# Two-block hybrid layer, dilated groups: value projection first in natural token tiles, through DRAM, ahead of keys and queries

## The chip, the cores and the metric

The kernel runs on one core of one Trainium2 chip. The metric is the device time of one execution in microseconds (us); lower is better. The kernel before takes 1719.8 us, the median of three runs (1716.84 to 1724.75).

## What is computed

The input is one sequence of 1024 tokens of width 1024, in float32. A first block (pooling and sliding-window attention) feeds a second, hybrid one. What matters here is the dilated attention of the second block: 24 heads of width 64 in three groups of eight. Queries, keys and values of a group are three slices of one projection, `h @ w_in`; queries and keys are rotated, values are not.

```
DIL_CONFIGS = ((128, 1), (512, 4), (2048, 16))

def dilated_mixture(q, k, v, positions):
    q = rope(q.reshape(B, S, DIL_HEADS, DIL_HEAD_DIM), positions)
    k = rope(k.reshape(B, S, DIL_HEADS, DIL_HEAD_DIM), positions)
    v = v.reshape(B, S, DIL_HEADS, DIL_HEAD_DIM)
    for g, (window, dilation) in enumerate(DIL_CONFIGS):
        sl = slice(g * DIL_HEADS_PER_GROUP, (g + 1) * DIL_HEADS_PER_GROUP)
        o, lse = dilated_group(q[:, :, sl], k[:, :, sl], v[:, :, sl], dilation, window // (2 * dilation))
    ...
    alpha = jax.nn.softmax(jnp.stack(lses, axis=0), axis=0)
    out = jnp.sum(alpha[..., None] * outs, axis=0)
```

In `dilated_group` a query sees the 64 keys of its own residue class on either side of it (dilation 1 or 4), or all 64 of its class (dilation 16).

## The kernel before, in words

The program is written by hand for the five engines, each with its own instruction stream and semaphores between them. Every float32 product is made of three passes: both operands are split into a high and a low part, and high times high, high times low and low times high are summed in PSUM.

The dilated part is a row of **units** (`D_UNITS`, L476). A unit is one 128x512 tile of a projection: 8 steps over the contraction, times three passes, so 24 matmuls, on TensorE (`d_proj`, L1172). For each group g there are eight units of keys, then those of values, then eight of queries. Keys and queries come out transposed (channels on partitions), 128 channels by 512 tokens. Values come out with tokens on partitions: the stationary operand is 128 columns of the transposed activations `h2T_hi` or `h2T_lo`, so the choice of columns chooses the tokens (`value_tiles`, L450). In group 0 the value tiles are shifted by 64 tokens against the query tiles, so that a query tile's window is two value tiles; that takes nine tiles for eight tiles' worth of tokens. In groups 1 and 2 a value tile's columns are taken with a step of 4 or 8 tokens.

A unit takes two **slots** (twelve matmuls each). `unit_before` (L508) tells which unit has just been finished at a slot. The three PSUM banks 0 to 2 take the units in turn (`d_bank`), and a unit waits until the one three before it has been read.

- A value unit is copied by ScalarE from PSUM to its tile in `v_dil` (L1756).
- A key or query unit is rotated. ScalarE copies it to `rope_in` (L1760). SyncE (SP) then issues four DMAs that write it to `rope_swapped` with 32-partition blocks exchanged (`swap_halves`, L599). VectorE multiplies the PSUM tile by the cosines into `kT_dil` or `qT_dil` (`rope_cos`, L2273), multiplies `rope_swapped` by the sines (L2280), and adds the two (`rope_sin`, L2284), which it tells by the semaphore `roped`. There is one `rope_in` and one `rope_swapped`: ScalarE's next copy waits for the swap before it, and the next swap waits for that add.

During the query units of a group the attention of that group runs in **steps** (`step_at`, L499), which begin `STEP_LAG` = 4 slots after the first query unit's own first slot: scores (`d_scores`, L1197), mask and maximum on VectorE, exponentials on ScalarE, transposes, and the product with the values (`d_values`, L1227, from `v_dil`). The last steps of a group lie beside the first three units of the next group. `d_scores` of a group's first step waits for `roped` of query unit 0 (groups 0 and 1) or 1 (group 2).

Weights come in **panels** of 512 columns, four chunks of 512 KB each. SP loads chunks (`load_chunk`, L630) into a ring of two, at the odd slots 1, 3, 5 and 7 of a panel; GpSimd splits each chunk into `w_hi` (L700) and `w_lo` (L707). There are two panels of split weights, so the splitting for the next panel begins when the one before the present is done, at the start of a panel of units. SP's stream is in program order: at the start of each panel it stands swap of the last unit, chunk load, swap of the next unit, chunk load, and so on.

After the dilated part the gates, the combination of the three groups, the latent attention and the output projections follow.

## Time and profile before

| what | before |
|---|---|
| median of the runs | 1719.8 us (1716.84 to 1724.75) |
| the profiled execution, its own time | 1716.44 us |
| its span from first to last instruction | 1714.6 us |
| TensorE matmul busy | 1686.5 us (98%), 8753 instructions |
| TensorE weight load busy | 1412.7 us (82%) |
| VectorE, ScalarE, GpSimd busy | 797.7, 586.1, 508.9 us |
| mean granted clock of TensorE | 0.999 of 2.4 GHz |

Of the 1716.44 us, 1.84 us lie around the span. The dilated units run from 558.75 us to about 1124 us of it. A busy matmul is not a matmul at its peak: the records overlap, so the pace is read from the distance of starts, not from durations.

### The profile page before, as it was taken

The numbers are of one execution on the slowest core, as the hardware profiler recorded it, in microseconds if no ns is written. First come the engines' busy times: TensorE is split into PE (matmuls) and PEld (weight loads), VectorE is DVE, ScalarE is ACT, GpSimd is POOL, SyncE is SP. The second block draws the span as 40 slices with busy tenths as digits, with TensorE's granted clock in tenths as the row PEclk, the third lists the DMA queues.
The fourth block names the chain that finished last, engine by engine and source line by source line (L and its number), as shares of the span: only waits on it lengthen the run. The fifth ranks groups of instructions, "written<-read, shape, count | busy, mean of one in ns | idle before, by whom it ended". The sixth has DMA issues, their size and how long they took to land.

```text
span 1714.6 us, 22451 instructions
## 1 busy us (share of the span) xinstructions
PE 1686.5 (98%) x8753; PEld 1412.7 (82%) x8753; DVE 797.7 (47%) x1214; ACT 586.1 (34%) x1337; POOL 508.9 (30%) x400
## 2 busy tenths in 40 slices
PE   7999999999999999999999999999999999999998
PEld 6778878889878787888978889788787999988886
DVE  4330366334342213554166541646521888855714
ACT  5101456334333102441134310442113777741211
POOL 6125033023333333021220223015313744534310
PEclk9999999999999999999999999999999999999999
DMA  6113022233267422113131232227465535226332
GB/s 205 50 65 108 13 62 70 87 119 93 74 215 269 117 62 59 50 50 85 56 84 38 72 83 60 69 54 267 137 227 164 139 63 139 53 68 212 107 114 98
DMA packets 99290, 178.20 MB, mean 104 GB/s; under 512 B 16200, under 2 KB 36080, under 8 KB 99056
## 3 DMA queue, kind: packets, MB, share of 16 engines
q1 hardware_dynamic: 63280, 95.31, 20.1%
q10 hardware_dynamic: 35904, 81.44, 13.5%
q8 instruction: 70, 1.15, 0.3%
q14 instruction: 36, 0.29, 0.1%
HBM read 115.49 MB, written 48.63 MB: 96 GB/s over the span
## 4 chain that ended last, share of the span: by engine, by line
PE 92%; DVE 2%; ACT 2%; DMA 1%; issue 1%; POOL 1%; SPq 1%; ACTq 0%; DVEq 0%; POOLq 0%
PE ps L1193 22%; PE ps L1107 15%; PE ps L813 13%; PE ps L1045 5%; PE ps L1360 5%; PE ps L1300 5%; PE ps L947 4%; PE ps L1241 4%; PE ps L1330 3%; PE ps L1313 3%; PE ps L868 3%; PE ps L1209 2%; PE ps L1222 2%; PE ps L999 2%; PE ps L972 1%
## 5 line engine op out<-in xcount | busy, mean ns | idle before, releaser
L700 POOL TENSOR_SCALAR w_hi<-w_stage 128x1024 fp32r<-128x1024 f32 (+3 forms) x140 | 127.5, 918 | 996.7 <-PE ps L1193 361.2
L707 POOL TENSOR_TENSOR w_lo<-w_stage,w_hi 128x1024 fp32r<-128x1024 f32 (+3 forms) x140 | 270.1, 1937 | 8.9
L1193 PE MATMUL ps<-h2T_hi,w_hi 128*128 128x512 f32 x384 | 156.7, 408 | 0.7 <-ACT gate_tiles L1608 0.7
L1107 PE MATMUL ps<-h2T_hi,w_hi 128*128 128x512 f32 x384 | 154.1, 401 | 0.5 <-issue 0.3
L1193 PE MATMUL ps<-h2T_hi,w_lo 128*128 128x512 f32 x384 | 152.2, 396 | 0.0
L1107 PE MATMUL ps<-h2T_lo,w_hi 128*128 128x512 f32 x384 | 151.8, 395 | 0.0
L1107 PE MATMUL ps<-h2T_hi,w_lo 128*128 128x512 f32 x384 | 151.6, 395 | 0.0
L1193 PE MATMUL ps<-h2T_lo,w_hi 128*128 128x512 f32 x384 | 151.3, 394 | 0.0
L1735 ACT ACTIVATE probs_dil<-probs_dil,dil_stats_out 128x256 f32<-128x256 f32 (+2 forms) x192 | 87.6, 457 | 137.1 <-DVE dil_stats_out L2301 137.1
L1300 PE MATMUL ps<-k_mla,q_mla 128*128 128x512 f32 x384 | 104.0, 406 | 0.0
L2393 DVE TENSOR_REDUCE small<-ps 128x1 f32<-128x1024 f32 x64 | 77.6, 1213 | 54.9 <-PE ps L1300 54.9
L2273 DVE SCALAR_TENSOR_TENSOR qT_dil<-ps,cos_table_T 128x512 f32<-128x512 f32 x24 | 23.1, 963 | 168.0 <-ACT rope_in L1760 168.0
L732 POOL TENSOR_SCALAR p_mla<-p_mla,small 128x1024 f32<-128x1024 f32 x64 | 71.7, 1120 | 88.1 <-DVE small L2386 87.9
L1193 PEld LDWEIGHTS ps<-h2T_hi,w_hi 128*128 128x128 f32 x384 | 72.1, 188 | 26.5 <-issue 9.2
L2380 DVE TENSOR_TENSOR pT_mla_lo<-ps,pT_mla_hi 128x512 fp32r<-128x512 f32 x128 | 81.9, 679 | 14.0 <-ACT pT_mla_hi L1848 14.0
L1848 ACT ACTIVATE pT_mla_hi<-ps 128x512 fp32r<-128x512 f32 x128 | 69.7, 596 | 52.1 <-PE ps L1313 52.1
L1107 PEld LDWEIGHTS ps<-h2T_hi,w_hi 128*128 128x128 f32 x384 | 72.2, 188 | 18.2 <-POOL w_lo L707 0.7
L1241 PEld LDWEIGHTS ps<-v_dil,probsT_dil 128*128 128x128 f32 (+1 forms) x640 | 80.6, 191 | 7.5 <-issue 1.1
L1193 PEld LDWEIGHTS ps<-h2T_hi,w_lo 128*128 128x128 f32 x384 | 72.2, 188 | 17.6
L1107 PEld LDWEIGHTS ps<-h2T_hi,w_lo 128*128 128x128 f32 x384 | 72.1, 188 | 17.6
L2280 DVE TENSOR_TENSOR rope_swapped<-rope_swapped,sin_table_T 128x512 f32<-128x512 f32 x48 | 43.6, 909 | 92.4 <-DMA rope_swapped<-rope_in 92.4
L1107 PEld LDWEIGHTS ps<-h2T_lo,w_hi 128*128 128x128 f32 x384 | 72.2, 188 | 16.3
(296 smaller groups left out, 3819.5 us busy)
## 6 DMA issues: line engine op xcount, KB each, us to landing
w_stage<-in_w_in SPq DMA_DIRECT2D x76, 512.0 KB, 3.9
rope_swapped<-rope_in SPq DMA_DIRECT2D x192, 64.0 KB, 2.0
w_stage<-in_w_out SPq DMA_DIRECT2D x16, 512.0 KB, 3.8
gate_scr<-gate_tiles ACTq DMA_DIRECT2D x16, 512.0 KB, 3.4
gates<-gate_scr ACTq DMA_DIRECT2D x32, 256.0 KB, 3.5
dil_scr<-dil_out SPq DMA_DIRECT2D x96, 64.0 KB, 1.6
dil_nums<-dil_scr ACTq DMA_DIRECT2D x24, 256.0 KB, 4.1
x_back<-in_x ACTq DMA_DIRECT2D x8, 512.0 KB, 3.9
```

The source lines that it names most:

```text
L700: last = nc.gpsimd.tensor_scalar(hi_, raw_, 1.0, 0.0, ALU.mult, ALU.add)
L707: last = nc.gpsimd.tensor_tensor(lo_, raw_, hi_.bitcast(F32), ALU.subtract)
L813: m = pe.matmul(acc, a, b, start=(i == 0 and j == 0), stop=(i == len(pairs) - 1 and j == 2))
L1045: m = pe.matmul(ps[:, Y_BANKS[t % 4] + half, :], a[:, k, tk], b[:, s, k, :], start=(k == 0 and j == 0), stop=(k == KT - 1 and j == 2))
L1107: m = pe.matmul(ps[:, gate_bank(u), :], a[:, s, k, P * m_:P * m_ + P], b[:, k, COLS * n:COLS * n + COLS], start=(k == 0 and j == 0), stop= ...
L1193: m = pe.matmul(bank, a, b, start=(k == 0 and i == 0), stop=(k == KT - 1 and i == 2))
L1241: m = pe.matmul(ps[:, 7, o:o + HD], pTd[r0:r0 + nr, c, :], vd[r0:r0 + nr, vt, HD * h:HD * h + HD], start=(kb == 0), stop=(kb == len(blocks ...
L1300: m = pe.matmul(ps[:, 2 * (i % 2) + n, :], Q[:, a, q], K[:, b, COLS * n:COLS * n + COLS], start=(j == 0), stop=(j == 2))
L1360: m = pe.matmul(ps[:, u % 8, :], a, b, start=(k == 0 and j == 0), stop=(k == 3 and j == 2))
L1735: act.activation(p_, p_, ACT.Exp, bias=o[:, h:h + 1], accum_out=o[:, H1 + h:H1 + h + 1]).then_inc(sem("d_exp"), 1)
L2380: nc.vector.tensor_tensor(PTl[dst], ps[:, 4 + half, :].rearrange("p (j c) -> p j c", c=P), PTh[dst].bitcast(F32), ALU.subtract).then_inc(s ...
L2393: nc.vector.tensor_reduce(rstd[:, j % 8:j % 8 + 1], ps[:, 2 * (j % 2):2 * (j % 2) + 2, :].rearrange("p b c -> p (b c)"), AX_X, ALU.max, ne ...
```

## The change

The order of a group is values, keys, queries. Value units are made in natural tiles (128 neighbouring tokens, 24 units in all instead of 25). ScalarE copies them to `rope_in` too. SP stores `rope_in` to a DRAM scratch `v_dil_scr` (256 KB, `store_values`), and ScalarE's next copy waits for that store. When all eight are stored, SP loads the tiles of `v_dil` that the attention reads from that scratch, one behind the swap of each key unit, with the shift or the step now in the rows that the load reads (`load_values`; 9, 8 and 8 loads of 256 KB). The first `d_values` of a group waits for these loads.

```diff
     for g in range(3):
+        add(f"v{g}", panel(w2, o_v + COLS * g))
         add(f"k{g}", panel(w2, o_k + COLS * g))
-        add(f"v{g}", panel(w2, o_v + COLS * g))
         add(f"q{g}", panel(w2, o_q + COLS * g))
...
+    vd_d = nc.dram_tensor("v_dil_scr", [S, 512], F32, kind="Internal").ap()
...
-    def value_tiles(g):
+    def value_rows(g):
 
         if g:
-            return [(t, group_toks(g, t)) for t in range(TT)]
-        starts = [0] + [P * t - HD for t in range(1, TT)] + [S - P]
-        return [(t, spread(s_, 1)) for t, s_ in enumerate(starts)]
+            return [tile_start(g, t) for t in range(TT)]
+        return [(0, 1)] + [(P * t - HD, 1) for t in range(1, TT)] + [(S - P, 1)]
...
-    D_UNITS = [(g, kind, t) for g in range(3) for kind in "kvq"
-               for t in range(len(value_tiles(g)) if kind == "v" else 2 * 4)]
+    D_UNITS = [(g, kind, t) for g in range(3) for kind in "vkq" for t in range(TT)]
...
+        def store_values(u):
+
+            g, _, t = D_UNITS[u]
+            sp.wait_ge(*after("d_read", u + 1))
+            if g and t == 0:
+                sp.wait_ge(*after("v_moved", 16 * (9, 17)[g - 1]))
+            sp.dma_start(vd_d[P * t:P * t + P, :], ts[:]).then_inc(sem("v_stored"), 16)
+
+        def load_values(u):
+
+            g, kind, t = D_UNITS[u]
+            for tile in range(t, TT + 1 if t == TT - 1 and g == 0 else t + 1):
+                sp.wait_ge(*after("v_stored", 16 * TT * (g + 1)))
+                if g:
+                    sp.wait_ge(*after("d_valued", d_step(g, 0)))
+                start, step = value_rows(g)[tile]
+                sp.dma_start(vd[:, tile, :], vd_d[start:start + step * (P - 1) + 1:step, :]).then_inc(sem("v_moved"), 16)
...
-            if done and done[3] != "v":
-                swap_halves(done[0])
+            if done:
+                (store_values if done[3] == "v" else swap_halves)(done[0])
+                if done[3] == "k":
+                    load_values(done[0])
...
                 if kind == "v":
-                    toks = value_tiles(g)[t][1]
-                    pairs = [(toks(a, k), b[:, s, k, :]) for a, b in ((h2h, wh), (h2h, wl), (h2l, wh))]
+                    pairs = [(a[:, k, P * t:P * t + P], b[:, s, k, :]) for a, b in ((h2h, wh), (h2h, wl), (h2l, wh))]
...
-                pe.wait_ge(*after("d_read", D_UNITS.index((g, "q", 0))))
+                pe.wait_ge(*after("v_moved", 16 * (9 + 8 * g)))
...
                 act.wait_ge(*after("d_done", u + 1))
-                if kind == "v":
-                    act.activation(vd[:, t, :], ps[:, d_bank(u), :], ACT.Copy).then_inc(sem("d_read"), 1)
-                else:
-                    if r:
-                        act.wait_ge(*after("swapped", 64 * r))
-                    act.activation(ts[:], ps[:, d_bank(u), :], ACT.Copy,
-                                   scale=HD ** -0.5 if kind == "q" else 1.0).then_inc(sem("d_copied"), 1)
+                if u and D_UNITS[u - 1][1] == "v":
+                    act.wait_ge(*after("v_stored", 16 * values_stored(u)))
+                elif u:
+                    act.wait_ge(*after("swapped", 64 * r))
+                act.activation(ts[:], ps[:, d_bank(u), :], ACT.Copy,
+                               scale=HD ** -0.5 if kind == "q" else 1.0).then_inc(sem("d_read" if kind == "v" else "d_copied"), 1)
```

On SP's queue, the end of group 0's key panel stands as follows before: the swaps of the last two key units, and then, without a further swap, the chunk loads that lie in the value panel; the swap of query unit 0 comes after them.

```order
L606 DMA rope_swapped<-rope_in 32x512 [waits roped,d_copied]
L606 DMA rope_swapped<-rope_in 32x512 x3
L606 DMA rope_swapped<-rope_in 32x512 [waits roped,d_copied]
L606 DMA rope_swapped<-rope_in 32x512 x3
L649 DMA w_stage<-in_w_in 128x2x512 [waits w_split] x5
L606 DMA rope_swapped<-rope_in 32x512 [waits roped,d_copied]
L606 DMA rope_swapped<-rope_in 32x512 x3
```

The same place in the change, from the swap of the last key unit on:

```order
L604 DMA rope_swapped<-rope_in 32x512 [waits roped,d_copied]
L604 DMA rope_swapped<-rope_in 32x512 x3
L622 DMA v_dil<-v_dil_scr 128x512 [waits rows_in7] x2
L665 DMA w_stage<-in_w_in 128x2x512 [waits w_split]
L604 DMA rope_swapped<-rope_in 32x512 [waits roped,d_copied]
L604 DMA rope_swapped<-rope_in 32x512 x3
L665 DMA w_stage<-in_w_in 128x2x512 [waits w_split]
```

Between the swap of the last key unit and that of query unit 0 stood the whole value panel; now two loads of value tiles and one chunk load stand there (`rows_in7` is the semaphore that carries `v_stored`).

On ScalarE, the copies of group 0 before: eight of keys, nine of values, and the first two of queries.

```order
L1760 ACTIVATE rope_in<-ps 128x512 [waits d_done]
L1760 ACTIVATE rope_in<-ps 128x512 [waits swapped,d_done] x7
L1756 ACTIVATE v_dil<-ps 128x512 [waits d_done,d_read]
L1756 ACTIVATE v_dil<-ps 128x512 [waits d_done] x8
L1760 ACTIVATE rope_in<-ps 128x512 [waits swapped,d_done] x2
```

And in the change:

```order
L1774 ACTIVATE rope_in<-ps 128x512 [waits d_done]
L1774 ACTIVATE rope_in<-ps 128x512 [waits rows_in7,d_done] x8
L1774 ACTIVATE rope_in<-ps 128x512 [waits swapped,d_done] x9
L1752 ACT_TABLE_LOAD
L1752 ACTIVATE probs_dil,dil_stats_out<-probs_dil,dil_stats_out 128x192 [waits row_max]
```

Nineteen copies before the first exponentials have become eighteen; eight of them (seven of values, and the first of keys) wait for a store, and the swaps' nine waits follow one another with no value copy in between.

## Rows read from the trace of the kernel before

**Rows 1.** The page: busy time, and the chain that ended last by engine.
```profile
PE 1686.5 (98%) x8753; PEld 1412.7 (82%) x8753; DVE 797.7 (47%) x1214; ACT 586.1 (34%) x1337; POOL 508.9 (30%) x400
...
PE 92%; DVE 2%; ACT 2%; DMA 1%; issue 1%; POOL 1%; SPq 1%; ACTq 0%; DVEq 0%; POOLq 0%
```
**Rows 2.** Busy time by stretch (value panels of groups 0 and 1): us, then each engine (instructions).
```profile
603.70:654.20 50.50, 50.50 (x217) 40.70 (x216) 6.09 (x5) 5.38 (x9) 14.47 (x8) 1.00 0.16 47
818.00:863.00 45.00, 45.00 (x193) 43.51 (x192) 2.71 (x3) 4.92 (x9) 14.49 (x9) 1.00 0.21 63
```
**Rows 3.** Line L1193, weight loads: min/median/max ns.
```profile
L1193 PEld LDWEIGHTS ps<-h2T_hi,w_hi x384: 185/188/201, 558.7 to 1118.2; 128*128 128x128 f32 x192
...
L1193 PEld LDWEIGHTS ps<-w_hi,h2T_hi x200: 186/311/337, 603.4 to 1054.6; 128*128 128x128 f32 x100
```
**Rows 4.** Timeline, ScalarE's copies of units: start us, us, engine, line, instruction, idle before.
```profile
564.65 0.60 ACT L1760 ACTIVATE rope_in<-ps 128x512 f32<-128x512 f32 x1 [5.95 <-PE ps L1193]
...
592.65 0.60 ACT L1760 ACTIVATE rope_in<-ps 128x512 f32<-128x512 f32 x1 [5.00 <-PE ps L1193]
...
615.09 0.60 ACT L1756 ACTIVATE v_dil<-ps 128x512 f32<-128x512 f32 x1 [4.96 <-PE ps L1193]
...
654.45 0.60 ACT L1756 ACTIVATE v_dil<-ps 128x512 f32<-128x512 f32 x1 [5.02 <-PE ps L1193]
...
821.82 0.60 ACT L1756 ACTIVATE v_dil<-ps 128x512 f32<-128x512 f32 x1 [3.69 <-PE ps L1193]
...
855.74 0.60 ACT L1756 ACTIVATE v_dil<-ps 128x512 f32<-128x512 f32 x1 [5.05 <-PE ps L1193]
```
**Rows 5.** Timeline, VectorE and ScalarE in the middle of key panels (groups 0, 1, 2).
```profile
586.40 0.69 DVE L2280 TENSOR_TENSOR rope_swapped<-rope_swapped,sin_table_T 128x512 f32<-128x512 f32 x1 [3.32 <-DMA rope_swapped<-rope_in]
591.74 0.69 DVE L2280 TENSOR_TENSOR rope_swapped<-rope_swapped,sin_table_T 128x512 f32<-128x512 f32 x1 [3.32 <-DMA rope_swapped<-rope_in]
...
789.72 0.60 ACT L1760 ACTIVATE rope_in<-ps 128x512 f32<-128x512 f32 x1 [8.96 <-DMA rope_swapped<-rope_in]
...
812.57 0.60 ACT L1760 ACTIVATE rope_in<-ps 128x512 f32<-128x512 f32 x1 [5.11 <-DMA rope_swapped<-rope_in]
...
989.49 0.60 ACT L1760 ACTIVATE rope_in<-ps 128x512 f32<-128x512 f32 x1 [9.84 <-DMA rope_swapped<-rope_in]
...
1012.87 0.60 ACT L1760 ACTIVATE rope_in<-ps 128x512 f32<-128x512 f32 x1 [5.24 <-DMA rope_swapped<-rope_in]
```
**Rows 6.** Timeline, GpSimd, VectorE and SP at the start of group 0's value panel.
```profile
603.90 1.05 POOL L700 TENSOR_SCALAR w_hi<-w_stage 128x1024 fp32r<-128x1024 f32 x1 [28.11 <-PE ps L1193]
605.03 2.71 POOL L707 TENSOR_TENSOR w_lo<-w_stage,w_hi 128x1024 fp32r<-128x1024 f32 x1
...
604.15 1.33 DVE L2280 TENSOR_TENSOR rope_swapped<-rope_swapped,sin_table_T 128x512 f32<-128x512 f32 x1 [3.32 <-DMA rope_swapped<-rope_in]
605.52 2.77 DVE L2284 TENSOR_TENSOR kT_dil<-kT_dil,rope_swapped 128x512 f32<-128x512 f32 x1
...
608.37 2.41 SPq L606 DMA_DIRECT2D rope_swapped<-rope_in  x4
```
**Rows 7.** Timeline, the start of group 1's query panel, up to its first scores.
```profile
855.79 1.06 POOL L700 TENSOR_SCALAR w_hi<-w_stage 128x1024 fp32r<-128x1024 f32 x1 [25.72 <-PE ps L1193]
856.93 2.40 POOL L707 TENSOR_TENSOR w_lo<-w_stage,w_hi 128x1024 fp32r<-128x1024 f32 x1
...
866.95 0.60 ACT L1760 ACTIVATE rope_in<-ps 128x512 f32<-128x512 f32 x1 [5.00 <-PE ps L1193]
...
868.39 3.44 SPq L606 DMA_DIRECT2D rope_swapped<-rope_in  x4
...
869.64 1.14 PE L1209 MATMUL ps<-kT_dil,qT_dil 64*128 64x256 f32 x8
```
**Rows 8.** The page, DMA issues: KB each, median us from issue to landing.
```profile
w_stage<-in_w_in SPq DMA_DIRECT2D x76, 512.0 KB, 3.9
...
pool_outT_back<-pool_scr ACTq DMA_DIRECT2D x8, 256.0 KB, 2.7
```

More of the change, by code:

```diff
@@ L125, in hybrid_blocks_kernel @@
         "values_copied": (("swa_out", 16), ("d_out", 48)),
-        "pool_in_out": (("pool_c", 80), ("pool_spill", 64)),
+        "pool_in_out": (("pool_c", 80), ("pool_spill", 64), ("v_moved", 400)),
     }
@@ L129, in hybrid_blocks_kernel @@
         shared[f"rows_in{t}"] = ((f"x_in{t}", 16),)
+    shared["rows_in7"] += (("v_stored", 16 * 3 * TT),)
     for b in range(2):
@@ L442, in tile_start @@
         return ((P * t, 1), (t // 2 + 4 * P * (t % 2), 4), (t, 8))[g]
-    def spread(start, step):
-        return lambda h, k: h[:, k, start:start + step * (P - 1) + 1:step]
-    def group_toks(g, t):
-        return spread(*tile_start(g, t))
-    def value_tiles(g):
+    def value_rows(g):
         if g:
-            return [(t, group_toks(g, t)) for t in range(TT)]
-        starts = [0] + [P * t - HD for t in range(1, TT)] + [S - P]
-        return [(t, spread(s_, 1)) for t, s_ in enumerate(starts)]
+            return [tile_start(g, t) for t in range(TT)]
+        return [(0, 1)] + [(P * t - HD, 1) for t in range(1, TT)] + [(S - P, 1)]
     def window(g, t):
@@ L482, in rope_units, with values_stored @@
         return sum(kind != "v" for _, kind, _ in D_UNITS[:u])
+    def values_stored(u):
+        return sum(kind == "v" for _, kind, _ in D_UNITS[:u])
     def d_step(g, i):
@@ L515, in d_bank @@
     def d_bank(u):
-        return (u + 2) % 3
+        return (u - N_D) % 3
     def gate_bank(u):
@@ L662, in load_chunk @@
                         sp.dma_start(edge[:, g, :], c_inv[g:g + 1, :].to_broadcast([P, PAD])).then_inc(sem("pool_c"), 16)
-        n = first_chunk["v0"] + STAGE
+        n = first_chunk["k0"] + STAGE
         load_chunks(0, n)
-        panel_start = {u: n + 4 * (index[f"{kind}{g}"] - index["k0"]) for u, (g, kind, t) in enumerate(D_UNITS) if t == 0}
+        panel_start = {u: n + 4 * (index[f"{kind}{g}"] - index["v0"]) for u, (g, kind, t) in enumerate(D_UNITS) if t == 0}
         place = 0
@@ L1749, in _ @@
                 u, r, g, kind, t = done
-                if kind == "v" and t == 0:
+                if kind == "v" and t == 0 and g:
                     act.wait_ge(*after("d_read", u))
-                    if g:
-                        act.wait_ge(*after("d_valued", d_step(g, 0)))
                 act.wait_ge(*after("d_done", u + 1))
-                if kind == "v":
-                    act.activation(vd[:, t, :], ps[:, d_bank(u), :], ACT.Copy).then_inc(sem("d_read"), 1)
-                else:
-                    if r:
-                        act.wait_ge(*after("swapped", 64 * r))
-                    act.activation(ts[:], ps[:, d_bank(u), :], ACT.Copy,
-                                   scale=HD ** -0.5 if kind == "q" else 1.0).then_inc(sem("d_copied"), 1)
+                if u and D_UNITS[u - 1][1] == "v":
[4 more added lines that the diff above has]
+                               scale=HD ** -0.5 if kind == "q" else 1.0).then_inc(sem("d_read" if kind == "v" else "d_copied"), 1)
             if slot in step_at:
@@ L2315, in _ @@
             if rope:
-                if done[4] == 0 and done[3] == "q":
+                if done[4] == 0 and done[3] == "k":
                     dve.wait_ge(*after("d_read", done[0]))
```

## The prediction

> **What bounds the kernel now.** The page first: TensorE is busy 98% of the span, and the chain that ended last lies on it for 92% [rows 1]. So an instruction taken from TensorE shortens the run by its pace, and the other engines count only where TensorE comes to wait for them. Then the timeline, for paces. ScalarE's copy of a unit starts as soon as the unit is finished. In group 0's key panel five units lie between the copies at 564.65 and 592.65: 5.60 us a unit. In its value panel seven units take 39.36 us (5.62 each), in group 1's, with its step of four tokens, six take 33.92 us (5.65 each) [rows 4]. TensorE never pauses in these panels [rows 2].
>
> The chain that the change touches is the rotation: copy, four swap DMAs, two VectorE operations, next swap. Its period must be set against the 5.60 us of a unit. In the middle of group 0's keys two sine multiplications lie 5.34 us apart: faster than TensorE. In group 1 four periods take 22.85 us (5.71 each), in group 2 23.38 us (5.85 each), and there ScalarE is released by the swap and not by TensorE [rows 5]. The key chain of groups 1 and 2 therefore falls behind, 0.12 and 0.25 us a unit. Now this costs nothing: the value panel behind it, with nothing to rotate, lets it catch up.
>
> **What is removed.** One value unit of group 0: 24 matmuls, 5.6 us. The sixteen value units of groups 1 and 2 become contiguous; by the 5.65 of the one and the 5.62 of the other [rows 4] that gives 0.03 us each, 0.5 us in all. Together **-6.1 us**. That their stationary loads fall from 311 to 188 ns [rows 3] is worth no more, as the 5.65 already includes them.
>
> **What is hidden.** 24 stores. One goes copy 0.6, issue about 0.4, then landing. A 256 KB DMA lands in 2.7 us here and a 512 KB one in 3.9 [rows 8], so 3.7 to 4.9 us, under the 5.6 of a unit; and three banks let ScalarE run late by more than a unit before TensorE waits. Behind ScalarE's new wait are queued, in the first three value units of groups 1 and 2, the exponentials of the last attention steps; a store that took longer than a unit would reach TensorE through them. The first product with values comes more than two units after the last load is issued. The attention's last steps now lie beside value units, which ask nothing of VectorE; no gain, since TensorE does not wait there.
>
> **What loses its cover.** Let T be the moment when the last key unit is copied; query unit 0 now comes next. By group 1, where T stands for 855.74 [rows 4] and the first scores start at 869.64 [rows 7], TensorE wants query unit 0 rotated at T+13.9 (groups 0 and 1), and query unit 1 at T+19.5 in group 2, one unit later. Before, the chain reached the query panel rested, and query unit 0 was rotated by 868.3 (the next swap, which waits for it, starts at 868.39 [rows 7]): 1.3 us to spare.
>
> It will reach it neither rested nor alone, for at T GpSimd begins to split the next panel's weights. Before, this was the start of the value panel: the sine multiplication of 604.15 falls into `w_hi` and takes 1.33 us instead of 0.69, the add of 605.52 falls into `w_lo` (605.03 to 607.74) and ends at 608.29, 0.55 behind it; the last key's swap starts only at 608.37 [rows 5, 6]. So I take it that a VectorE operation that falls into a split ends 0.55 us behind it (0.95 for the add of groups 1 and 2, which is strided). The Trainium skill, "SBUF — State Buffer", section "Who interferes with whom", has this as a rule: a VectorE instruction with two SBUF inputs and a GpSimd instruction that reads SBUF share an exclusive port pair, and the later one blocks. It speaks against this change; without it, the walks below would give less than half of their stalls.
>
> Now the walk. By the splits that begin at 855.79 [rows 7], GpSimd works at T+0.05 to 1.1 and 1.2 to 3.6 (first chunk), 3.6 to 4.6 and 4.7 to 7.1 (second); the third chunk waits for SP. From the start of a swap to the sine multiplication I take 3.85 us (the period of 5.71, less both operations and the handing over, about 1.86).
> - *Group 0.* No lag. Swap T+0.6, multiplication T+4.5, blocked to 5.1, add blocked to about T+8.0. Swap of query 0 at 8.1, rotated at T+13.4. Wanted at 13.9: **stall 0**.
> - *Group 1.* The first key unit meets splits as query unit 0 did before, where the next swap started at 868.39 rather than 867.55, the end of the copy that starts at 866.95 [rows 7]: lag 0.85. With five times 0.12 the last but one key lags 1.45. Its multiplication comes at T+0.3, blocked to 1.6, and its add to T+4.85. Last key's swap 4.95, rotated 10.6; query 0's swap 10.65, multiplication 14.5. SP could load the third chunk only at T+7.9; it is split from 11.8 to 15.4, which blocks to 15.9. Rotated at T+17.0: **stall 3.1** (2.3 if that split is missed).
> - *Group 2.* The same walk with five times 0.25: last key's swap T+5.0, query 0's 10.8, query 1's 17.2, rotated at T+23.0; wanted at 19.5: **stall 3.5** (2.8).
>
> The loads of values are new traffic behind each key's swap. Below, they cost nothing: issued at 2.4 us of a period of 5.7, a load has landed when the next swap has scarcely begun. Above, each holds up the next swap by what 256 KB add to a landing, 1.2 us [rows 8]. I take 0.1 us a unit, near the lower end, since the chunk loads at the same place left the period of group 0 under 5.6; it adds about **0.6 us** in all, as splits swallow part of it.
>
> **Sum.** -6.1 + 0 + 3.1 + 3.5 + 0.6 = +1.1 us. Profiled execution: 1716.4 + 1.1 = 1717.5. It ran 3.4 us under the median of the runs, so against 1719.8 I give **1720.9 us**. A measurement can tell about 0.5% (8.6 us) from no change.
>
> **Rivals.**
> 1. *The rotation keeps up.* The splits are met at other moments, or the chain makes up its lag, and only the removal is left: 1719.8 - 6.1 = 1713.7. For it: 1.3 us to spare, and group 0 needs no stall. Against it: the periods of 5.71 and 5.85, and that the splitting begins with TensorE's own last key unit.
> 2. *Slower: the value loads get in front of the swaps.* The place is SP's queue in the key panels. At 1.2 us a unit the periods are 6.54, 6.91 and 7.05; eight units (nine in group 2) fall behind by 7.5, 10.5 and 13.1 us, and less the 1.7, 1.3 and 1.3 to spare (group 0's adds are 0.4 shorter) TensorE stalls 27 us: 1719.8 - 6.1 + 27 = 1740.7. Half that delay a unit is the point from which the loss passes 8.6 us, counting the splits. For it: 256 KB of load and 512 KB of weights now follow each of the first swaps. Against it: the same weights alone didn't disturb group 0.
> 3. *Weight loads set the pace.* In group 1's value panel they are busy 43.5 of 45.0 us, in group 0's 40.7 of 50.5 [rows 2]. If each of the 384 strided loads gave back its 0.122 us [rows 3], 46.8 us and the unit's 5.6 would go: 1667. Against it: the pace of 5.65 beside 5.62. The Trainium skill, "Perfetto Trace Analysis", section "Identifying the Most-Contended Engine", would have TensorE judged by the busy share of its weight loads and not of its matmuls; the paces here do not bear it out.
>
> That the change doesn't remove the unit is excluded: its instruction list on TensorE is 24 matmuls shorter.
>
> **Chances.** My forecast (stalls that eat about what the unit gives) 0.64; rival 1 0.23; rival 2 0.10; rival 3 0.01; something unseen 0.02. The forecast's own range is 1716 to 1726. Rival 1, with the spread of the runs, takes the lower end to 1713, and part of rival 2 the upper to 1729. Faster by over 0.5% (under 1711.2) 0.07: rival 3, and rival 1 where the runs fall low. Slower by over 0.5% (over 1728.4) 0.12: rival 2, and a bad case of the forecast. Within: 0.81.
>
> **What would show it.** Matmuls 8729. Value units at 5.62 us or less in all groups, their weight loads at 188 ns. No pause in the value panels. In the first query units, TensorE idle before the first scores (L1209 before), released by VectorE's add: near 0 in group 0, 2 to 4 us in groups 1 and 2. VectorE's rotation operations at the start of query panels at 1.3 to 3.3 us. The swaps' landing still near 2 us. I am wrong if the first scores start without a wait (rival 1), if the key chain's period is over 6.2 us (rival 2), or if the value units go under 5.5 us (rival 3).

## The result, and the profile after

The changed kernel took **1727.54 us** (median of 8 runs, 1724.82 to 1729.33), the kernel before 1718.84 us in the same measurement; the ratio is 1.0055, 95% interval 1.0046 to 1.0065. It is slower by 0.46 to 0.65%, some 9 us. The forecast was 1720.9, with a full range of 1713 to 1729 and an own range of 1716 to 1726; the result lies inside the first and 1.5 us above the second. The profiled execution took 1727.61 us with a span of 1725.8, against 1716.44 and 1714.6 before.

First the page of the changed kernel: busy times, and the chain that ended last by engine (beside [rows 1]).

```profile
PE 1684.3 (98%) x8729; PEld 1391.4 (81%) x8729; DVE 789.9 (46%) x1214; ACT 586.0 (34%) x1336; POOL 510.1 (30%) x400
...
PE 85%; DVE 6%; DMA 3%; SPq 3%; ACT 2%; issue 1%; POOL 0%; ACTq 0%; DVEq 0%; POOLq 0%
...
rope_swapped<-rope_in SPq DMA_DIRECT2D x192, 64.0 KB, 2.0
...
v_dil<-v_dil_scr SPq DMA_DIRECT2D x25, 256.0 KB, 3.1
v_dil_scr<-rope_in SPq DMA_DIRECT2D x24, 256.0 KB, 2.0
```

TensorE has 24 matmuls fewer. But the chain lies on it for 85% instead of 92%; VectorE, DMA and SP have what is gone. Where it waits, the list of waits shows, over the dilated part (560 to 1190 us of the span): what waited, for whom, us in total, times, longest.

```profile
PE ps L1226 <- DVE qT_dil L2298: 11.0, 2, 6.1
PE ps L1226 <- DVE probs_dil L2308: 2.8, 7, 0.7
...
PE ps L1239 <- ACT probs_dil L1752: 0.4, 1, 0.4
```

The same list of the kernel before has no wait for a rotated query tile at all:

```profile
PE ps L1222 <- ACT probs_dil L1735: 1.1, 2, 0.8
PE ps L1209 <- DVE probs_dil L2294: 0.7, 2, 0.4
```

The two long waits are the first scores of groups 1 and 2. Group 0 has none, as forecast. Here is the whole chain of group 1 in the timeline (VectorE, GpSimd, SP and TensorE; rows of other work left out). T, the end of the last key unit on TensorE, is 850.85 (the unit copied at 811.6, and seven units of 5.60).

```profile
850.89 1.05 POOL L718 TENSOR_SCALAR w_hi<-w_stage 128x1024 fp32r<-128x1024 f32 x1 [27.36 <-PE ps L1210]
852.02 2.40 POOL L725 TENSOR_TENSOR w_lo<-w_stage,w_hi 128x1024 fp32r<-128x1024 f32 x1
853.07 1.89 DVE L2294 TENSOR_TENSOR rope_swapped<-rope_swapped,sin_table_T 128x512 f32<-128x512 f32 x1 [2.92 <-DMA rope_swapped<-rope_in]
...
855.00 1.80 DVE L2298 TENSOR_TENSOR kT_dil<-kT_dil,rope_swapped 128x512 f32<-128x512 f32 x1
...
856.88 2.41 SPq L604 DMA_DIRECT2D rope_swapped<-rope_in  x4
...
859.38 0.53 SPq L622 DMA_DIRECT2D v_dil<-v_dil_scr  x1
...
859.95 0.46 SPq L665 DMA_DIRECT2D w_stage<-in_w_in  x1
...
862.60 2.41 SPq L604 DMA_DIRECT2D rope_swapped<-rope_in  x4
...
865.02 1.04 POOL L718 TENSOR_SCALAR w_hi<-w_stage 128x1024 fp32r<-128x1024 f32 x1 [5.94 <-DMA w_stage<-in_w_in]
...
866.14 2.34 POOL L725 TENSOR_TENSOR w_lo<-w_stage,w_hi 128x1024 fp32r<-128x1024 f32 x1
866.50 2.53 DVE L2294 TENSOR_TENSOR rope_swapped<-rope_swapped,sin_table_T 128x512 f32<-128x512 f32 x1 [2.99 <-DMA rope_swapped<-rope_in]
...
868.94 1.04 POOL L718 TENSOR_SCALAR w_hi<-w_stage 128x1024 fp32r<-128x1024 f32 x1 [0.45 <-DMA w_stage<-in_w_in]
869.07 1.82 DVE L2298 TENSOR_TENSOR qT_dil<-qT_dil,rope_swapped 128x512 f32<-128x512 f32 x1
...
870.94 2.08 PE L1226 MATMUL ps<-kT_dil,qT_dil 64*128 64x256 f32 x8 [6.15 <-DVE qT_dil L2298]
```

Read it from the top: the multiplication of the last but one key comes at T+2.2 and is stretched from 0.69 to 1.89 by GpSimd's split; the last key's swap starts at T+6.0, query unit 0's at T+11.75; its multiplication and its add meet the next two splits (2.53 and 1.82), and it is rotated at T+20.0. TensorE had wanted it at T+13.9. In group 2 the first scores, which need query unit 1, wait 4.82 us in the same way:

```profile
1082.21 1.23 PE L1226 MATMUL ps<-kT_dil,qT_dil 64*128 64x128 f32 x8 [4.82 <-DVE qT_dil L2298]
```

The granted clock of TensorE in group 1, in stretches of 2 us (columns: stretch, length, busy time and instructions of PE, PEld, DVE, ACT, POOL, then the clock, the DMA share and GB/s):

```profile
868.00:870.00 2.00, 0.00 (x0) 0.00 (x0) 1.97 (x2) 0.00 (x0) 1.53 (x2) 0.50 0.13 49
870.00:872.00 2.00, 1.06 (x6) 0.89 (x8) 1.88 (x2) 0.00 (x0) 1.94 (x1) 0.50 0.00 0
...
876.00:878.00 2.00, 2.00 (x8) 1.29 (x7) 1.37 (x2) 1.79 (x8) 0.00 (x0) 0.68 0.33 127
878.00:880.00 2.00, 2.00 (x16) 1.44 (x16) 0.92 (x2) 0.00 (x0) 0.00 (x0) 1.00 0.00 0
```

After the wait TensorE works at the lower level, 1.2 GHz, for some 6 us, and is back at 2.4 GHz at 878. In group 2 it does so for some 3 us (0.52 granted in 1082 to 1084, 0.63 in 1084 to 1086, then 1.00). The experiments below say what that costs.

For the kernels in the changed order I measure, in the profiled runs, two things. The columns of the groups go from ScalarE's copy of key unit 0 to that of query unit 7. The column "on TensorE" goes from the first to the last projection matmul of the whole dilated part; there the kernel before takes 560.2 us.

| kernel | group 0 | group 1 | group 2 | sum | on TensorE | median of its runs |
|---|---|---|---|---|---|---|
| the change | 130.4 | 137.5 | 114.4 | 382.3 | 569.6 | 1727.54 |
| k2, late splits | 130.1 | 130.3 | 116.4 | 376.8 | 565.4 | 1724.31 |
| k3, filled wait | 130.2 | 136.6 | 115.3 | 382.1 | 568.9 | 1726.80 |
| k4, two queues | 130.1 | 128.9 | 105.1 | 364.1 | 553.3 | 1709.57 |
| k7, loads twice | 140.5 | 138.5 | 120.4 | 399.5 | 586.8 | 1738.59 |
| k8, two queues and late splits | 130.1 | 128.6 | 113.0 | 371.7 | 560.8 | 1718.94 |
| k9, half the issues | 130.1 | 128.9 | 104.2 | 363.2 | 552.4 | 1709.08 |
| k10, late splits in group 1 | 130.4 | 130.0 | 113.8 | 374.2 | 561.6 | 1719.55 |
| k11, loads early | 136.7 | 133.6 | 114.6 | 384.9 | 572.2 | 1727.66 |

The medians come from four measurements; in these the kernel before took 1718.84 (the change), 1717.39 (k1 to k4), 1716.84 (k5 to k8) and 1716.16 us (k9 to k11). By their ratios to it, the change stands at 1.0055 and k4 at 0.9956: 0.99%, 17 us, apart. On TensorE they differ by 16.4 us (k9 and the change by 17.3), in the sums by 18.2. The sums say too much in group 2, because there ScalarE's copy of query unit 7 stands behind the exponentials of the attention steps and not directly behind TensorE. k5 shows it: it puts the quick swap of k4 into the kernel before, the last copy comes 2.2 us earlier after that of group 1 (175.7 instead of 177.9 us), and the whole is no faster. So the columns are good for seeing where something is lost, and "on TensorE" for how much.

### The profile page after: what moved, and what is told of

Same layout as the page of the kernel before. It is cut to its first block, busy times and chain, and to the rows that moved or that the text cites. A ratio compares the mean times of both kernels' runs of the same rounds, so it can differ in the third digit from the quotient of the medians.

```text
span 1725.8 us, 22489 instructions
## 1 busy us (share of the span) xinstructions
PE 1684.3 (98%) x8729; PEld 1391.4 (81%) x8729; DVE 789.9 (46%) x1214; ACT 586.0 (34%) x1336; POOL 510.1 (30%) x400
## 4 chain that ended last, share of the span: by engine, by line
PE 85%; DVE 6%; DMA 3%; SPq 3%; ACT 2%; issue 1%; POOL 0%; ACTq 0%; DVEq 0%; POOLq 0%
PE ps L1210 15%; PE ps L1125 14%; PE ps L831 14%; PE ps L1063 5%; PE ps L1377 5%; PE ps L1317 5%; PE ps L965 4%; PE ps L1258 4%; PE ps L1347 4%; PE ps L1330 3%; DMA rope_swapped<-rope_in 3%; PE ps L886 3%; SPq L604 3%; PE ps L1226 2%; PE ps L1239 2%; DVE rope_swapped L2294 2%
## 5 line engine op out<-in xcount | busy, mean ns | idle before, releaser
L1774 ACT ACTIVATE rope_in<-ps 128x512 f32<-128x512 f32 x72 | 42.8, 595 | 265.2 <-PE ps L1210 155.6
L1125 PEld LDWEIGHTS ps<-h2T_hi,w_hi 128*128 128x128 f32 x384 | 72.1, 188 | 17.3 <-issue 0.4
```

Of the source, the lines that this page charges most:

```text
L1125: m = pe.matmul(ps[:, gate_bank(u), :], a[:, s, k, P * m_:P * m_ + P], b[:, k, COLS * n:COLS * n + COLS], start=(k == 0 and j == 0), stop= ...
```

## Experiments

**Where the swap's time goes: two queues.** `k4_two_queues`: ScalarE, which has just copied the tile, issues two of the four swap DMAs.

```diff
-            for b in range(4):
+            for b in range(2):
                 sp.dma_start(rot[32 * b:32 * b + 32, :], ...)
...
+                if kind != "v":
+                    act.wait_ge(*after("d_copied", r + 1))
+                    if r:
+                        act.wait_ge(*after("roped", r))
+                    for b in range(2, 4):
+                        act.dma_start(rot[32 * b:32 * b + 32, :], ts[32 * (b ^ 1):32 * (b ^ 1) + 32, :]).then_inc(sem("swapped"), 16)
```

> The change, with two of the four swap DMAs of each rotated unit issued by ScalarE, so that the issue of a swap takes 1.2 us instead of 2.4. Theory A (the chain's period of 5.7 and 5.85 us against a unit's 5.6 builds the lag): the period falls to about 4.6 us, so the chain is never late in the key panels, and one collision with a split at the end fits into what is spare: waits before the first scores under 1 us, 1711 to 1715 us, faster than the kernel before. Theory B (value loads): the loads still follow each swap, the gain is 3 us at most: 1724 us or more. Against the gain: ScalarE now waits for VectorE's add before it issues, which could delay exponentials in the query panels.

Measured: 1709.57 us, ratio 0.9956 (0.9944 to 0.9969). It beats both kernels, and lies 1.4 us below the range of theory A. The middle of group 1's key panel, first in the changed kernel (timeline; the swap row there is one of the slow ones, its like at 831.03 took 2.41):

```profile
834.87 0.69 DVE L2294 TENSOR_TENSOR rope_swapped<-rope_swapped,sin_table_T 128x512 f32<-128x512 f32 x1 [2.92 <-DMA rope_swapped<-rope_in]
834.93 0.60 ACT L1774 ACTIVATE rope_in<-ps 128x512 f32<-128x512 f32 x1 [5.13 <-DMA rope_swapped<-rope_in]
835.60 1.08 DVE L2298 TENSOR_TENSOR kT_dil<-kT_dil,rope_swapped 128x512 f32<-128x512 f32 x1
...
836.75 3.38 SPq L604 DMA_DIRECT2D rope_swapped<-rope_in  x4
```

And k4, at the same place:

```profile
832.55 0.60 ACT L1774 ACTIVATE rope_in<-ps 128x512 f32<-128x512 f32 x1 [5.00 <-PE ps L1210]
833.18 1.14 SPq L604 DMA_DIRECT2D rope_swapped<-rope_in  x2
833.18 1.41 ACTq L1781 DMA_DIRECT2D rope_swapped<-rope_in  x2
...
836.04 0.69 DVE L2300 TENSOR_TENSOR rope_swapped<-rope_swapped,sin_table_T 128x512 f32<-128x512 f32 x1 [1.72 <-DMA rope_swapped<-rope_in]
```

The sign to look for is what ends ScalarE's idle time (after `<-`). In the change the copy waits for the swap, so the loop through the one `rope_swapped` tile sets the pace; in k4 it waits for TensorE, every 5.60 us. From the start of a swap to the multiplication k4 needs 2.86 us (833.18 to 836.04) where the change needs 3.84 (831.03 to 834.87). The Trainium skill, "DMA: Bandwidth & Descriptors", section "Issuing engines are not separate DMA queues", says that issuing on several engines saves only the sequencer's time, "usually small relative to the DMA itself". The transfers indeed get no faster (landing 2.0 us on SP, 2.2 on ScalarE); but here that sequencer time, 2.41 us for four, is over half of the time from a swap's start to the multiplication, and taking half of it away was worth 17 us.

**Is it the second queue, or fewer issues in a row?** `k9_half_the_issues` keeps one queue and issues two transfers of 64 partitions.

```diff
-            for b in range(4):
-                sp.dma_start(rot[32 * b:32 * b + 32, :], ts[32 * (b ^ 1):32 * (b ^ 1) + 32, :])...
+            for b in range(2):
+                sp.dma_start(rot[64 * b:64 * b + 64, :], ts[64 * (b ^ 1):64 * (b ^ 1) + 64, :])...
...
-                    act.wait_ge(*after("swapped", 64 * r))
+                    act.wait_ge(*after("swapped", 32 * r))
...
```

> The changed kernel with the swap of a key or query tile issued as two transfers of 64 partitions on SyncE instead of four of 32; the same bytes move, but halves of 64 rows change place instead of blocks of 32, so keys and queries are rotated with the wrong partner rows. Theory A (the loop of copy, swap, multiplication and add is 5.7 to 5.85 us long in groups 1 and 2 because SyncE's four issues take 2.41 us of it; that it is longer than a unit's 5.6 is what makes the stalls): with 1.2 us of issue the loop is some 4.7 us, ScalarE's copies are released by TensorE again, and the time is that of k4_two_queues, 1709 to 1713. Theory B (what helped there was the second queue, the transfers travelling beside each other): 1722 or more.

Measured: 1709.08 us, ratio 0.9959 (0.9947 to 0.9972). Theory A: the same bytes on the same queue, in half the issues (1.10 us instead of 2.41), remove the stalls. TensorE's waits for a rotated query tile fall from 11.0 us to 0.3.

**Does the kernel before gain from it?** `k5_before_two_queues` is k4's edit on the kernel before.

> The kernel before, with two of the four swap transfers of each key and query tile issued by ScalarE instead of SyncE. Theory A: in the order keys, values, queries TensorE waits only some 3 us in all between the value panel and the last scores, so there is nothing for the faster swap to give back: 1716 to 1718, within 1 us of the kernel before; then what k4_two_queues gained (7.8 us) is the change's own gain once its stalls are gone. Theory B: the second queue is a gain by itself: 1711 or less.

Measured: 1717.51 us, ratio 1.0006 (0.9997 to 1.0014). No gain, as theory A says. The quick swap is worth nothing where the values stand behind the keys and 17 us where the queries do. So k4's 7.8 us below the kernel before are the change's own gain, freed of its stalls.

**What does that gain consist of?** The sum had 6.1 us for it. `k6_before_contiguous` reads the value tiles of groups 1 and 2 in natural order in the kernel before.

```diff
-            return [(t, group_toks(g, t)) for t in range(TT)]
+            return [(t, spread(P * t, 1)) for t in range(TT)]
```

> The kernel before with the token tiles of the values of groups 1 and 2 read in natural order (step 1) instead of step 4 and step 8, nothing else changed; this changes which tokens these value tiles hold, so the output is that of another assignment of tokens. Theory A: the stationary reads with step 8 are what makes the 8 value units of group 2 take 5.88 us where the contiguous ones take 5.61, those with step 4 5.65: the time falls by 8 x 0.04 + 8 x 0.27 = 2.5 us, to about 1715, and the units' copies come 5.61 us apart. Theory B (the sum of the prediction, 0.5 us for both groups; the slower pace of group 2 has another cause): 1717, and the copies of group 2 stay 5.88 apart.

Measured: 1714.57 us, ratio 0.9990 (0.9981 to 0.9998), 2.3 us between the medians. Group 2's value copies in the timeline of ScalarE, first in the kernel before:

```profile
1020.53 0.60 ACT L1756 ACTIVATE v_dil<-ps 128x512 f32<-128x512 f32 x1 [1.59 <-PE ps L1193]
...
1055.76 0.60 ACT L1756 ACTIVATE v_dil<-ps 128x512 f32<-128x512 f32 x1 [5.29 <-PE ps L1193]
```

And k6:

```profile
1019.63 0.60 ACT L1756 ACTIVATE v_dil<-ps 128x512 f32<-128x512 f32 x1 [0.99 <-PE ps L1193]
...
1053.37 0.60 ACT L1756 ACTIVATE v_dil<-ps 128x512 f32<-128x512 f32 x1 [5.03 <-PE ps L1193]
```

Six units take 35.23 us before (5.87 each) and 33.74 in k6 (5.62 each). A step of 8 tokens (32 bytes) costs 0.25 us a unit, one of 4 tokens 0.03 to 0.04. Theory A holds; with the 5.6 us of the unit removed the change gives back about 8 us, which is what k4 shows (7.8 by the medians, 6.9 on TensorE).

**GpSimd's splits.** `k2_late_splits`: in the query panels GpSimd waits until query unit 1 is rotated before it splits the next weights, and SP loads their chunks four units later.

```diff
-            if (slot - place) % 2 and (slot - place) // 2 < 4 and u < N_D:
-                load_chunk(start + (slot - place) // 2)
+            late = 4 if D_UNITS[min(u, N_D - 1)][1] == "q" else 0
+            if (slot - place) % 2 and 0 <= (slot - place) // 2 - late < 4 and u < N_D:
+                load_chunk(start + (slot - place) // 2 - late)
...
+            for g in range(3):
+                if p == index[f"q{g}"] + 1:
+                    pool.wait_ge(*after("roped", 16 * g + 8 + 2))
```

> The change, but in query panels GpSimd begins to split the next panel's weights only when query unit 1 is rotated, and SP loads the four chunks in units 4 to 7 instead of 0 to 3. Theory A (lag plus collisions of VectorE's rotation with the splits): the operations at the start of the query panels are back at 0.69 and 1.08 us, the waits before the first scores shrink from 11.0 us in all to 2 to 4 us, too short for the clock to fall: 1714 to 1719 us. Theory B (value loads hold up the swaps): the loads are all still there, the waits stay at 8 us or more: 1724 us or more.

Measured: 1724.31 us, ratio 1.0042 (1.0030 to 1.0055). The time is theory B's, but not its reason: the value loads are all there, and the waits for a rotated query tile still fell from 11.0 to 2.8 us, as theory A says. What came instead are waits for the masks, 8.6 us instead of 2.8. By the table group 1 gained 7.2 us and group 2 lost 2.0. Group 2's timeline in k2 shows the splits falling on the next query tile:

```profile
1075.79 2.65 POOL L726 TENSOR_TENSOR w_lo<-w_stage,w_hi 128x1024 fp32r<-128x1024 f32 x1
1076.28 3.10 DVE L2302 TENSOR_TENSOR qT_dil<-qT_dil,rope_swapped 128x512 f32<-128x512 f32 x1
1079.30 0.74 DVE L2312 TENSOR_TENSOR probs_dil<-ps,masks 128x256 f32<-128x256 f32 x2
...
1080.10 1.22 PE L1230 MATMUL ps<-kT_dil,qT_dil 64*128 64x128 f32 x8 [4.09 <-DVE probs_dil L2312]
```

The add takes 3.10 us, the mask of the attention step stands behind it in VectorE's order, and TensorE waits 4.09 us for that. `k10_late_split_group1` makes the same two edits in group 1 alone.

> The changed kernel with GpSimd's splits held back, and their chunks loaded later, in the query panel of group 1 alone; groups 0 and 2 as in the change. Theory A (the 7.2 us that group 1 gained in k2_late_splits stay gained, and group 2's loss there was its own): 1727.5 - 7.2 = 1720.3, range 1719 to 1722, and group 2's time from its last key to its last query unit stays at 75.2 us. Theory B (a group that ends its stall earlier meets the next wait elsewhere, so that the gain is given back): 1724 or more.

Measured: 1719.55 us, ratio 1.0014 (1.0001 to 1.0027), within theory A's range. Group 1 takes 130.0 us instead of 137.5, and the gain is kept to the end (8.0 us on TensorE). Group 2 stayed near the change's 114.4 (113.8). In its list of waits two waits for query tiles are left, 6.1 us in all, of which group 2's is 4.9:

```profile
PE ps L1229 <- DVE qT_dil L2301: 6.1, 2, 4.9
```

`k8_two_queues_late_splits` puts k2's edits on k4.

> The changed kernel with both edits: two swap transfers of four on ScalarE's queue, and GpSimd's splits of the next weight chunks held back in the query panels. Theory A (k4_two_queues had removed all stalls but some 4 us of small ones; the late splits only move the collision of VectorE with GpSimd to another tile): 1709 to 1713, not under k4. Theory B (the collision still costs at the panel's start even with two queues): 1706 to 1708.

Measured: 1718.94 us, ratio 1.0014 (1.0006 to 1.0022): worse than both theories, 9 us over k4. Groups 0 and 1 are as good as in k4; group 2 takes 113.0 instead of 105.1, and TensorE waits 8.0 us in six pieces there, for the masks. Behind the last projection it takes 3.7 us more than k4 in the profiled runs. The multiplication at 1090.65 takes 2.89 us beside `w_lo`:

```profile
1090.59 2.40 POOL L726 TENSOR_TENSOR w_lo<-w_stage,w_hi 128x1024 fp32r<-128x1024 f32 x1
1090.65 2.89 DVE L2304 TENSOR_TENSOR rope_swapped<-rope_swapped,sin_table_T 128x512 f32<-128x512 f32 x1 [0.59 <-DMA rope_swapped<-rope_in]
```

Late splits are bad in group 2 whatever the swap does: a multiplication or an add that is stretched there stands ahead of a mask that TensorE waits for. I had not counted that.

**The lower clock.** `k3_filled_wait` keeps TensorE busy with 26 (group 1) and 22 (group 2) products of no use ahead of the first scores.

```diff
+            if i == 0 and g:
+                pe.wait_ge(*after("d_out", n))
+                for w in range({0: 0, 1: 26, 2: 22}[g]):
+                    pe.matmul(ps[:, 7, :], h2h[:, w % KT, 0:P], h2h[:, w % KT, 0:COLS], start=True, stop=True)
```

> The change, with 26 (group 1) and 22 (group 2) idle-filling matmuls of 512 columns between the last projection matmul and the first scores of the group; they write a bank that nobody reads before it is written again, and take about 6.1 and 5.1 us, as long as TensorE waits there now. Nothing of the computation changes. Theory A (about 4.5 us of the 15.5 that the order costs are matmuls at 1.2 GHz behind the wait): the granted clock stays at full speed, and the time falls from 1727.5 to 1723 us (1722 to 1725). Rival (the clock's fall costs nothing that the wait did not cost already): 1727 us or more.

Measured: 1726.80 us, ratio 1.0058 (1.0046 to 1.0071), mean granted clock 0.998 instead of 0.994; group 1 took 136.6, group 2 115.3, in sum as before. That is the rival: the change's ratio is 1.0055. The wait is filled, and the clock stays at its upper level:

```profile
863.53 6.08 PE L1220 MATMUL ps<-h2T_hi 128*128 128x512 f32 x26
869.83 1.13 PE L1230 MATMUL ps<-kT_dil,qT_dil 64*128 64x256 f32 x8 [0.23 <-DVE qT_dil L2302]
```

The scores come no sooner to their softmax for it. The fillers (11.2 us) and the waits for query tiles (1.4), masks (4.0) and exponentials (1.1) make 17.7 us; the same waits of the change make 14.2 (11.0, 2.8 and 0.4). As k3 is only 0.7 us shorter on TensorE, the matmuls at the lower clock had taken some 4.2 us more (an estimate from these figures), and 3.5 of them come back as waits. So the slow stretch after the stall costs next to nothing by itself: most of what it takes from TensorE, TensorE would have waited for the softmax.

**The value loads.** `k1_values_between` goes back to keys, values, queries, keeps the natural tiles and the scratch, and loads the values where it can: in group 0 in the value panel, in groups 1 and 2 partly there and partly in a burst of four behind query unit 0.

```diff
-    D_UNITS = [(g, kind, t) for g in range(3) for kind in "vkq" for t in range(TT)]
+    D_UNITS = [(g, kind, t) for g in range(3) for kind in "kvq" for t in range(TT)]
...
+            elif g == 1 and kind == "v" and t >= 4:
+                tiles = (2 * (t - 4),)
+            elif g == 1 and kind == "q" and t == 0:
+                tiles, stored = (1, 3, 5, 7), TT
...
+            elif g == 2 and kind == "v" and t == TT - 1:
+                tiles, stored = (0, 1, 2, 3), TT
+            elif g == 2 and kind == "q" and t == 0:
+                tiles, stored = (4, 5, 6, 7), TT
```

> The change with its order of units put back to keys, values, queries; natural value tiles and the way through DRAM are kept (24 stores, 25 loads), and the loads now lie in the value panel and behind the first query unit. Theory A (the value panel was the cover in which the rotation chain caught up; the way through DRAM itself costs nothing): no wait before the first scores beyond 0.5 us, clock at full speed throughout, and only the removed unit is left: about 1718.8 - 6.1 = 1712.7 us (1711 to 1715). Theory B (the stores or loads of values, their traffic or SP's time, are the cost): no better than the kernel before, 1719 us or more.

Measured: 1720.10 us, ratio 1.0018 (1.0009 to 1.0027). Theory A's numbers are missed; the time is theory B's, 1719 or more. Group 1's first scores did start without a wait, but those of groups 0 and 2 waited 1.4 and 2.4 us, and the waits for masks are 6.8 us in all. In group 1 the burst stands in front of the next swap (timeline, SP and VectorE):

```profile
861.04 1.97 SPq L635 DMA_DIRECT2D v_dil<-v_dil_scr  x4
863.06 0.42 SPq L678 DMA_DIRECT2D w_stage<-in_w_in  x1
864.83 2.41 SPq L604 DMA_DIRECT2D rope_swapped<-rope_in  x4
...
871.14 0.69 DVE L2306 TENSOR_TENSOR rope_swapped<-rope_swapped,sin_table_T 128x512 f32<-128x512 f32 x1 [1.16 <-DMA rope_swapped<-rope_in]
871.87 3.09 DVE L2310 TENSOR_TENSOR qT_dil<-qT_dil,rope_swapped 128x512 f32<-128x512 f32 x1
```

From swap to multiplication it takes 6.31 us instead of 3.85, then the add meets a split, and the second scores wait 3.06 us. The order alone is not to be judged by this run: it moved the loads, and what they cost, to another place. What it shows is that four loads and a chunk in front of a swap delay it.

`k7_loads_twice` issues each load of value tiles 0 to 7 a second time, into a tile that lies idle. The first attention step of a group then waits for these loads too.

```diff
+                if tile < TT:
+                    if g or tile:
+                        sp.wait_ge(*after("v_extra", 16 * (8 * g + tile)))
+                    sp.dma_start(prd1[:, 0:2, :].rearrange("p a c -> p (a c)"), vd_d[start:...:step, :]).then_inc(sem("v_extra"), 16)
...
```

> The changed kernel, each of its value loads of groups' tiles 0 to 7 issued twice (24 more transfers of 256 KB out of the scratch, into a tile that lies idle then), each just behind a key's swap. Theory A (the 25 value loads themselves cost little; the stall is made by the softmax steps that follow the key panel too closely, and the loads only delay a swap where they stand in front of it): 1727 to 1731. Theory B (the surplus of 17 us over the stall-free time is paid by the loads in proportion): 25 loads cost most of 17 us, 24 more another 12 or so: 1738 or more.

Measured: 1738.59 us (four runs), ratio 1.0129 (1.0114 to 1.0143). The number is theory B's, but by the table (its profiled execution took 1742.54 us, 4 over the median) not for its reason: 10.2 us are new in group 0, which had no stall to pay in proportion, 6.0 in group 2 and only 1.0 in group 1. `k11_loads_early` moves the single loads, two behind each of the first four keys.

```diff
-            for tile in range(t, TT + 1 if t == TT - 1 and g == 0 else t + 1):
+            for tile in range(min(2 * t, TT), 2 * t + 2 + (t == 3 and g == 0) if t < 4 else TT):
```

> The changed kernel with its value loads two behind each of the first four key tiles' swaps instead of one behind each of the eight, so that none stands near the last keys or the first queries. Theory A (the single loads cost nothing where they stand; the loop is too long by itself and GpSimd's splits do the rest): 1726 to 1729, group 1 from its last key to its last query unit 96 to 98 us. Theory B (the loads are what took the stalls from the predicted 3.1 and 3.5 us to 8.9 and 8.0): 1720 or less.

Measured: 1727.66 us, ratio 1.0066 (1.0054 to 1.0079). The sum is theory A's, but group 1 was better than it said (94.4 us from T to the copy of the last query unit, for 96 to 98; the change takes 98.3): 3.9 us gained there, 6.3 lost in group 0. There the second key's multiplication meets a split for 2.56 us (1.20 in the change), and two loads are issued right behind the third swap:

```profile
622.53 2.41 SPq L604 DMA_DIRECT2D rope_swapped<-rope_in  x4
...
624.99 1.94 SPq L622 DMA_DIRECT2D v_dil<-v_dil_scr  x2
...
628.15 0.69 DVE L2294 TENSOR_TENSOR rope_swapped<-rope_swapped,sin_table_T 128x512 f32<-128x512 f32 x1 [5.09 <-DMA rope_swapped<-rope_in]
```

It takes 5.62 us from swap to multiplication instead of 3.83 (group 0 of the change); the last of its four transfers lands 3.8 us after its issue, where 2.0 is usual. Group 0's chain, which had kept up, is late, and its first scores wait 3.8 us. So one load behind a swap costs little in the middle of a panel, two in the first half are too many (how much of it is the split and how much the loads isn't separated), and near the last keys of group 1 the single ones are worth up to 3.9 us. What the loads cost the changed kernel in all is not settled: every variant that moved them paid elsewhere.

## Why the forecast was right, and where it was not

*What happens* was right at each place. The unit is gone (8729 matmuls); value units run at 5.62 us with loads of 188 ns in all groups; value panels have no pause; group 0 does not stall; groups 1 and 2 stall at the first scores, for 6.1 and 4.8 us where 2 to 4 were given, released by VectorE's add, because the rotation reaches the query panel late and meets the splits. In the middle of group 2's keys the period is still 5.85 us with the loads behind the swaps, so rival 2 did not come about.

*The sizes* were wrong at two terms, in opposite directions.

1. **The removal**, -6.1: the step "by the 5.65 of the one and the 5.62 of the other ... 0.03 us each" priced sixteen strided units by group 1 alone. Group 2's take 5.87. With 8 x 0.03 and 8 x 0.25 the term is -7.8; k6 measured the stride part, k4 the whole. A sentence of mine even had the hint, the weight loads of 311 ns in the median and 337 at most [rows 3]: I took one group for both. What rival 3 looks for is real in group 2, for 2 us and not for 46.8. The busy share of the weight loads would not have told it: they are busy without a gap in group 1 (838 to 843) as in group 2 (1040 to 1045), with a matmul every 235 ns in the one and every 245 ns in the other (the 43.5 of 45.0 us of [rows 2] take in key and query units at the ends). That it is the step, k6 shows. Why the wider step costs so much more than the narrower stays open.

```profile
838.00:843.00 5.00, 5.00 (x23) 5.00 (x22) 0.00 (x0) 0.60 (x1) 0.00 (x0) 1.00 0.00 0
...
1040.00:1045.00 5.00, 5.00 (x22) 5.00 (x21) 0.00 (x0) 0.60 (x1) 0.00 (x0) 1.00 0.00 0
```

2. **The stalls**, 3.1, 3.5 and 0.6, in sum 7.2. Against k4 they cost 16.4 us on TensorE: 0.3 in group 0, 8.8 in group 1 and 7.3 in group 2 (against k9, with its even quicker group 2, 17.3). The groups are parted here at ScalarE's copy of the fifth value unit, which TensorE releases in both kernels (587.80, 789.16 and 996.16 in the change). The walk fell short in three ways that the trace shows:
 - *The lag.* It had 1.45 us on the last but one key of group 1, and its multiplication at T+0.3. It came at T+2.2. One swap was issued in 3.38 us instead of 2.41 (836.75, above), and another multiplication, at 822.45, the second key's, took 1.62 instead of 0.69 as it met a split: 1.9 us together, and nothing gives back a lag in a loop that is longer than a unit. The slow issue was to be seen before as well, with 3.44 us [rows 7]; I had taken the usual value.
 - *The third chunk.* SP loaded it at T+9.1, not T+7.9, it landed later than the 3.9 us assumed, and its split began only at T+14.2 instead of T+11.8: just when query unit 0 was multiplied, and the fourth one met its add. The walk had it rotated at T+17.0; it was T+20.0. The method fell short here, not the rule: a collision that is missed by a microsecond in the walk costs two to three here. The 0.55 us rule held: `w_lo` ended at 868.48, the multiplication at 869.03.
 - *What follows the first wait.* The walk stopped at the first scores. The waits for them are 11.0 us, and 5.4 more are lost behind them: by the estimate from k3 some 4.2 by matmuls at the lower clock, in stretches where the attention steps, begun late, would have held TensorE anyway, and the rest by waits for masks. k10 shows that this is bound to its group: 7.5 us of group 1 come back when the splits of its query panel are held back.

How much of the 16.4 is owed to the term of 0.6 us, the value loads, is not known, as said above; a load landed in 3.1 us at the median, where the walk took 2.7.

On TensorE the dilated part went from 560.2 to 569.6 us: k4 stands 6.9 us below the kernel before, and the stalls put 16.4 on top, which makes +9.5. The medians differ by 8.7 us, the profiled spans by 11.2, of which 1.7 lie outside this part. So the forecast of +1.1 had both sizes too small, the gain by 1.7 us (7.8 for 6.1) and the loss by 9.2 (16.4 for 7.2).

That the result still fell into the full range is partly luck. It lies above the forecast's own 1726, in the part up to 1729 that had been added for rival 2, which did not come about; the error in the gain took back 1.7 us, and the kernel before ran at 1718.84 in this measurement; on the 1719.8 that I had counted from, the same ratio makes 1729.3, just outside. It is also at the edge of what I had called no change: under the 1728.4, but with 0.55% just over the half per cent.

## What to carry to other kernels

When a panel is moved, look for a loop whose period is just above the pace that feeds it and ask which panel let it rest. A fixed small lag costs nothing in front of work that does not use the loop, and everything in front of work that waits for it. Then count the issues within such a loop before its bytes: here a second queue, or half as many transfers, turned some 9 us of loss into 8 us of gain, and did nothing at all where the loop had its rest. Walk a stall past its first wait, and take the slow instances of an issue into account, not its median.

## What the hardware showed that I had not expected

- The step of the stationary operand, in fp32 and 128 columns: weight loads of 188 ns contiguous, some 309 with a step of 16 bytes, some 331 with one of 32; but the matmuls' pace only 234, 235 and 245 ns (a unit's 5.62, 5.65 and 5.87 us through 24). With either step the recorded loads leave no gap, so their busy share does not tell the two paces apart.
- Four DMA issues of 64 KB take SP 2.41 us as a rule, and now and then 3.2 to 3.5 (3.38 at 836.75), with the same transfers; in a closed loop such a slip is kept.
- Half the transfers at double the partitions (k9) and two queues (k4) are worth the same to 0.5 us (1709.08 and 1709.57 us, in two measurements): it is the issuing that a 64 KB swap waits for here.
- TensorE working at 1.2 GHz, for some 6 us behind group 1's stall and some 3 behind group 2's, cost nothing that could be measured (k3: ratio 1.0058 with the clock kept up, 1.0055 without), as most of it would have been spent waiting for the softmax.
